# Hybrid layer kernel: V kept unsplit and split chunk by chunk, three ring slots for the remainders

## The chip, the cores and the metric

One core of a Trainium2 chip runs the whole layer in one launch. The metric is the device time of one execution in microseconds (us). The engines are named as in the profile: PE is the matrix engine (PEld its weight loads), DVE, ACT and POOL work on tiles, SP issues most of the DMAs. SBUF is the memory on the chip, PSUM the accumulators that PE writes, DRAM the memory outside.

## The reference, cut to what matters

A layer over 2048 rows of width 1024 in float32. `proj = x @ w_in` gives queries, keys, values and gates for four branches; stick-breaking attention is the first of them. For each head (4 heads of 128) and each block of 128 queries:

```
z      = q @ k^T * scale                       # 128 queries x keys up to the diagonal
log_1m = log_sigmoid(-z), 0 above the diagonal
w      = exp(log_sigmoid(z) + sum of log_1m over the later keys)
o      = w @ v
```

The kernel computes the same as products: the share of a key is sigmoid(z), the remainder is the running product of sigmoid(-z) over the later keys, w is share times remainder. The other branches (pooling, a gated recurrence, cross attention to a memory), the gated sum of the branches, `merged @ w_out` and a layer norm are untouched by the change.

## The kernel before, in words

Float32 products are made of three faster ones: every operand is split into a high part (a rounding copy, by ACT) and a low part (operand minus high, by DVE or POOL), and PE adds high x high, high x low and low x high (`pass3`, lines 821 to 825).

The rows are worked on in two halves of 1024 columns (`half`). Projections are made two tiles at a time: a pair `g` (36 in each half) is 14 pieces `i` of six matmuls of 512 columns. Pairs 0 to 7 of a half give the heads' q, k, v and gate; the odd pair of a head gives v. Every engine's program is written out by hand, and every engine walks the same list of pieces in the same order; semaphores tie them together.

**V before.** In the odd pair of a head, at pieces 10 and 12, PE turns half of V (4 transposes of 128x128 into a PSUM bank, `turn`, line 890), ACT copies the high part out (`values_hi`, line 1277), DVE makes the low part (`turned`, line 1755). SP stores both parts in `pk_v` in DRAM (`keep_values`). A chunk of 512 keys comes back with both parts as 512 KB in one DMA into `VC` (`load_v`, line 518), after the values product of the chunk before it has read `VC`.

**The attention.** `attention(half, h)` walks steps `s`, 12 a head in half 0 and 28 in half 1. A step is one block of 128 queries against one chunk of 512 keys (fewer on the diagonal); four steps make a group that reads one chunk of keys and one of values. In iteration `s` PE does `scores(s)` (into one of two PSUM banks), some pieces of projections of the next pairs as filling, in iterations 4n+7 and 4n+8 the two products with values of group n, and last `turned(s - 3)`, the transposes of the weights. The others, by iteration:

- ACT: the high part of the turned weights of step s-4 (line 1380), `shares(s)` (`KEEP` line 1366, `SHARE` line 1371), filling.
- DVE: `remainder(s - 1)`, the scan that writes `REST` (line 1901), the mask on diagonals (1890), the low part of the turned weights of step s-4 (1914), in one iteration of each head the first output (`Y<-AO,Y`, line 1921; iteration 9 in half 0, 17 in half 1), filling (among it lines 1746, 1777, 1784).
- POOL: `weights(s - 1)`, REST times SHARE in place (line 2390), filling (lines 2333, 2341, 2320).

`scores(s + 2)` writes the bank that the scan of step s reads (its first column stands in as the unused second operand) and waits for it: `wait_if(pe, scan_done, gs - 1)`. `REST` has four slots, one for each query block of the group; the scan of a step starts from the last element of its own slot, written four steps earlier, and waits until PE has turned the step before it in the same slot: `wait_if(dve, wt_done, gs - BLOCKS + 1)`.

Of the kernel before, what the change touches and what calls it, by code (L numbers as in the profile page):

```python
# [11 lines left out]
P = 128  # L12
# [70 lines left out]
TURN, TAIL = 3, 5  # L83
# [29 lines left out]
def first_step(half, h):  # L113
    return half * HEADS * NS[0] + h * NS[half]

# [60 lines left out]
def build(nc, xt, xrow, memt, w8, w4, wgate, wpool, prm, cst, ln_g, ln_b, out):  # L176
    with ExitStack() as ctx:
# [24 lines left out]
        B = R + 48.03125  # L202
# [23 lines left out]
        REST = at("REST", R + 32, [BLOCKS, C + 2])  # L226
        WTH = at("WTH", R + 40.03125, [2, BLOCKS, HALF], F32R)
        KC = [at(f"KC{i}", R + 48.03125 + 4 * i, [2, C], F32R) for i in range(2)]
        KEEP = at("KEEP", R + 56.03125, [2, C + 2])
        WTL = at("WTL", R + 60.0625, [2, BLOCKS, HALF], F32R)  # L230
        VC = at("VC", R + 68.0625, [BLOCKS, 2, P], F32R)
# [20 lines left out]
        LR_ = [at(f"LR{i}", R + k, [T]) for i, k in enumerate((28, 8, 52.0625))]  # L252
# [3 lines left out]
        LG = [at(f"LG{i}", R + 52.0625 + 4 * i, [T]) for i in range(2)]  # L256
        LA, LT = at("LA", R + 60.0625, [T]), at("LT", R + 64.0625, [T])
# [38 lines left out]
        pk_v = nc.dram_tensor("pk_v", (HEADS, P, SEQ // P, 2, P), F32).ap()  # L296
# [33 lines left out]
        v_kept = [sem("v_hi_kept"), sem("v_lo_kept")]  # L330
# [3 lines left out]
        v_tr, v_hi, v_blk = sem("v_tr"), sem("v_hi"), sem("v_blk")  # L334
# [122 lines left out]
        def _(sp):  # L457
# [35 lines left out]
            def keep_values(g):  # L493
                half, h = g // PAIRS, g % PAIRS // 2
                hh = half * HEADS + h
                for part, of in ((1, places(half, STL)[1]), (0, places(half, STL)[2])):
                    sp.wait_ge(v_blk, 2 * hh + 2)
                    sp.dma_start(pk_v[h, :, half * TB:(half + 1) * TB, part, :],
                                 of[:].bitcast(F32).rearrange("p (b m) -> p b m", m=P)).then_inc(v_kept[part], 16)
# [9 lines left out]
            def load_v(half, h, i):  # L509

                n, k = first_group(half, h) + i, STEPS[half][BLOCKS * i][1]
                if i == 0:
                    for kept in v_kept:
                        sp.wait_ge(kept, 16 * (half * HEADS + h + 1))
                    if h == 0:
                        wait_if(sp, o_out[1], 16 * 3 * half)
# [24 lines left out]
            def attention(half, h):  # L541
# [3 lines left out]
                for s in range(ns + TAIL + 1):  # L545
# [11 lines left out]
                    elif BLOCKS < s <= ns and s % BLOCKS == 0:  # L557
                        load_v(half, h, s // BLOCKS - 1)
# [260 lines left out]
        def _(pe):  # L819
# [16 lines left out]
            def piece(g, i, ks=(0, 1)):  # L836
# [9 lines left out]
                elif i == 0:  # L846
                    pe.wait_ge(a_lo, g + 1)
                    wait_if(pe, ad_done, 4 * (g - 1) + 2)
                    if 2 <= l <= 2 * HEADS and l % 2 == 0:
                        pe.wait_ge(v_blk, 2 * (half * HEADS + l // 2))  # L850
# [27 lines left out]
                if l < 2 * HEADS and l % 2 and i in (10, 12):  # L878
                    turn(g, 0 if i == 10 else 1)

            def turn(g, part):

                hh = g // PAIRS * HEADS + g % PAIRS // 2
                v, c = places(g // PAIRS, ST)[2], J[(g + 1) % 2]
                if part:
                    pe.wait_ge(v_blk, 2 * hh + 1)
                else:
                    pe.wait_ge(ad_done, 4 * g + 2)
                for j in range(4):
                    mm = nc.tensor.transpose(c[:, j * P:(j + 1) * P], v[:, (4 * part + j) * P:(4 * part + j + 1) * P],  # L890
                                             IDENT[:])
                mm.then_inc(v_tr, 1)
# [47 lines left out]
            def turned(half, h, s):  # L940
# [5 lines left out]
                n = C - a  # L946
                for b in range(n // P):
                    w = REST[:, j, n - P * (b + 1):n - P * b]
# [3 lines left out]
            def values(half, h, i):  # L952
# [6 lines left out]
                pe.wait_ge(v_in, 16 * (n + 1))  # L959
# [182 lines left out]
        def _(act):  # L1142
# [32 lines left out]
            def room(g, p):  # L1175
# [3 lines left out]
                if kind == "head":  # L1179
# [3 lines left out]
                    if i % 2 == 0 and p:  # L1183
                        wait_if(act, v_kept[1], 16 * hh)
# [4 lines left out]
                    elif i % 2:  # L1189
                        wait_if(act, v_kept[0], 16 * hh)  # L1190
                elif kind == "merge" and i >= 2:
                    gates_read(half, n, 2 * i + p - 4)
                elif kind == "merge" and n == 0:
                    if i == 0:
# [3 lines left out]
                        elif half or not p:  # L1198
                            act.wait_ge(k_kept, 32 * HEADS * (half + 1))
                            act.wait_ge(v_kept[1], 16 * HEADS * (half + 1))  # L1200
                        else:
                            act.wait_ge(v_kept[0], 16 * HEADS * (half + 1))
                    elif p:
                        act.wait_ge(w_done, S_END[half])
                    elif half:
                        act.wait_ge(v_kept[0], 16 * HEADS * (half + 1))
# [38 lines left out]
            def piece(g, i):  # L1245
# [24 lines left out]
                if g % PAIRS < 2 * HEADS and g % 2 and i in (10, 12):  # L1270
                    values_hi(g, 0 if i == 10 else 1)

            def values_hi(g, part):

                hh = g // PAIRS * HEADS + g % PAIRS // 2
                act.wait_ge(v_tr, 2 * hh + part + 1)
                nc.scalar.copy(places(g // PAIRS, STL)[2][:, part * C:(part + 1) * C], J[(g + 1) % 2][:]).then_inc(v_hi, 1)
# [121 lines left out]
            def attention(half, h):  # L1399
# [8 lines left out]
                for s in range(ns + TAIL + 1):  # L1408
                    if 0 <= s - TURN - 1 < ns:
                        turned_hi(half, h, s - TURN - 1)  # L1410
# [1146 lines left out]
```

## Time and profile before

| | us |
|---|---|
| median of 3 runs | 2293.88 (2293.3 to 2294.76) |
| the profiled execution | 2293.96 |
| its span in the trace | 2292.2 |
| PE busy | 2279.5 (99%) |
| DVE busy | 1444.4 (63%) |
| POOL busy | 1224.3 (53%) |
| ACT busy | 1060.2 (46%) |
| DMA moved | 297.84 MB, mean 130 GB/s |

The profiled execution has 1.8 us around its span and stands 0.1 us above the median. PE shows busy almost throughout, but its records overlap (matmuls are pipelined), so its pace is read from the starts of successive matmuls. Time of another engine counts only where PE waits for it. The attention takes the span from 79 to 285 us in half 0 and from 1144 to 1473 us in half 1.

### The profile page before, as it was taken

To read this page: it belongs to the slowest core of one execution; us is meant where nothing else is said; L and a number is where in the kernel's file an instruction comes from. 1 tells how busy PE (TensorE), PEld (TensorE's weight loads), DVE (VectorE), ACT (ScalarE), POOL (GpSimd) and SP (SyncE) were. 2 spreads that over 40 slices of the span, in tenths; PEclk is the share of its full clock that TensorE was granted. 3 is DMA by queue.
4 is the path that set the end of the run, shared out by engine and by line. 5 is a ranking of instruction groups with operands and counts; after the bars stand their busy time and mean duration, and the time that the engine had idled before them with its cause. 6 is when DMAs were issued, how large, how long until landed. Compare 5 with 4: busy or idle time off the path is not lost.

```text
span 2292.2 us, 29991 instructions
## 1 busy us (share of the span) xinstructions
PE 2279.5 (99%) x10824; PEld 1886.8 (82%) x10824; DVE 1444.4 (63%) x1658; ACT 1060.2 (46%) x1627; POOL 1224.3 (53%) x847
## 2 busy tenths in 40 slices
PE   9999999999999999999999999999999999999998
PEld 6888888888878888888888888888888778888887
DVE  7565542764496478568877777733854585486476
ACT  5555542343385255332576676632342583355220
POOL 1666643865456355435476566644863556456341
PEclk9999999999999999999999999999999999999999
DMA  6544422123334345373344543322133334354442
GB/s 234 187 159 158 139 83 97 55 83 129 113 104 133 134 124 148 105 284 138 108 159 139 165 156 124 125 92 78 56 120 124 92 103 134 130 156 132 152 161 83
DMA packets 114419, 297.84 MB, mean 130 GB/s; under 512 B 11232, under 2 KB 41056, under 8 KB 113248
## 3 DMA queue, kind: packets, MB, share of 16 engines
q1 hardware_dynamic: 112544, 290.68, 38.6%
q10 hardware_dynamic: 1728, 5.24, 0.7%
q8 instruction: 87, 1.43, 0.3%
q14 instruction: 60, 0.49, 0.1%
HBM read 216.19 MB, written 71.30 MB: 125 GB/s over the span
## 4 chain that ended last, share of the span: by engine, by line
PE 97%; DVE 1%; DMA 1%; issue 0%; DVEq 0%
PE J L823 21%; PE J L825 21%; PE J L824 21%; PE ZZ L995 8%; PE AO L995 8%; PE ZZ L825 2%; PE ZZ L824 2%; PE ZZ L823 2%; PE AO L825 2%; PE AO L824 2%; PE AO L823 2%; PE AO L949 1%; PE JX L949 1%; PE ZZ L1030 1%; PE JX L825 1%; PE JX L823 1%
## 5 line engine op out<-in xcount | busy, mean ns | idle before, releaser
L2341 POOL TENSOR_TENSOR WLS<-SR,WHS 128x512 fp32r<-128x512 f32 x264 | 414.3, 1588 | 110.1 <-ACT WHS L1161 102.5
L823 PE MATMUL J<-XBH,WHS 128*128 128x512 f32 x1152 | 452.3, 393 | 0.0
L825 PE MATMUL J<-XBH,WLS 128*128 128x512 f32 x1152 | 449.1, 390 | 0.0
L824 PE MATMUL J<-XBL,WHS 128*128 128x512 f32 x1152 | 448.9, 390 | 0.0
L823 PE MATMUL J<-XBH,WH 128*128 128x512 f32 x864 | 340.3, 394 | 0.4 <-DVE WL L1764 0.2
L825 PE MATMUL J<-XBH,WL 128*128 128x512 f32 x864 | 337.0, 390 | 0.0
L824 PE MATMUL J<-XBL,WH 128*128 128x512 f32 x864 | 336.8, 390 | 0.0
L825 PEld LDWEIGHTS J<-XBH,WLS 128*128 128x128 f32 x1152 | 216.2, 188 | 46.0
L824 PEld LDWEIGHTS J<-XBL,WHS 128*128 128x128 f32 x1152 | 216.4, 188 | 43.6 <-issue 0.2
L823 PEld LDWEIGHTS J<-XBH,WHS 128*128 128x128 f32 x1152 | 216.4, 188 | 43.5 <-issue 0.2
L2333 POOL TENSOR_TENSOR SR<-RAW 128x512 f32<-128x512 f32 x71 | 100.6, 1417 | 269.8 <-DMA RAW<-w 230.8
L1746 DVE TENSOR_TENSOR ST<-J,ST 128x512 f32<-128x512 f32 x160 | 109.5, 685 | 209.1 <-PE J L825 162.2
L2390 POOL TENSOR_TENSOR REST<-REST,SHARE 128x512 f32<-128x512 f32 (+3 forms) x160 | 165.6, 1037 | 119.7 <-DVE REST L1901 116.1
L2407 POOL TENSOR_TENSOR BL<-BRAW,BH 128x512 fp32r<-128x512 f32 x64 | 89.3, 1401 | 220.2 <-ACT BH L1429 220.0
L823 PEld LDWEIGHTS J<-XBH,WH 128*128 128x128 f32 x864 | 162.3, 188 | 40.1 <-issue 7.3
L1161 ACT CAST WHS<-SR 128x1024 fp32r<-128x1024 f32 x144 | 151.3, 1051 | 93.5 <-POOL SR L2333 92.4
L825 PEld LDWEIGHTS J<-XBH,WL 128*128 128x128 f32 x864 | 162.2, 188 | 34.8
L824 PEld LDWEIGHTS J<-XBL,WH 128*128 128x128 f32 x864 | 162.3, 188 | 31.8 <-issue 0.2
L2333 POOL TENSOR_TENSOR SR<-SR,RAW 128x512 f32<-128x512 f32 x71 | 105.6, 1488 | 120.4 <-PE J L825 118.4
L1243 ACT COPY ST<-J 128x512 f32<-128x512 f32 x160 | 93.8, 590 | 125.1 <-PE J L825 122.4
L1901 DVE TENSOR_TENSOR_SCAN REST<-KEEP,REST,ZZ 128x513 f32<-128x513 f32 x96 | 122.8, 1279 | 25.5 <-ACT SHARE L1371 24.6
L2333 POOL TENSOR_TENSOR SR<-RAW,SR 128x512 f32<-128x512 f32 x71 | 102.3, 1441 | 51.3 <-PE J L825 50.3
(305 smaller groups left out, 4753.3 us busy)
## 6 DMA issues: line engine op xcount, KB each, us to landing
RAW<-w SPq DMA_DIRECT2D x144, 512.0 KB, 3.7
pk_m<-MB SPq DMA_DIRECT2D x56, 512.0 KB, 5.0
MB<-pk_m SPq DMA_DIRECT2D x48, 512.0 KB, 3.9
KC<-pk_k SPq DMA_DIRECT2D x40, 512.0 KB, 5.4
VC<-pk_v SPq DMA_DIRECT2D x40, 512.0 KB, 4.4
BRAW<-w SPq DMA_DIRECT2D x64, 256.0 KB, 5.0
XRAW<-xt SPq DMA_DIRECT2D x8, 1024.0 KB, 12.6
pk_v<-STL SPq DMA_DIRECT2D x16, 512.0 KB, 5.0
```

The source lines that it names most:

```text
L823: nc.tensor.matmul(to, wh, xh, start=first, stop=True, skip_group_check=True)
L824: nc.tensor.matmul(to, wh, xl, start=False, stop=True, skip_group_check=True)
L825: return nc.tensor.matmul(to, wl, xh, start=False, stop=True, skip_group_check=True)
L995: mm = nc.tensor.matmul(BR[p][c][:], w[p][:, k, :], y[k][:, c * C:(c + 1) * C], start=(k == 0 and m == 0), stop=(k == KB - 1 and m == 2))
L1161: nc.scalar.copy(WHS[:, k, :], SR[:, k, :]).then_inc(w_hi, 1)
L1243: nc.scalar.copy(dest(g)[p][:, c * C:(c + 1) * C], J[(g + bank) % 2][:]).then_inc(cp_done, 1)
L1746: V_.tensor_tensor(d, bank[:], d, ALU.add).then_inc(ad_done, 1)
L1901: V_.tensor_tensor_scan(REST[:, j, 0:n + 1], KEEP[:, gs % 2, 0:n + 1], ZB[gs % 2][:, 0:1].broadcast_to([P, n + 1]), 1.0 if diag else REST[ ...
L2333: G_.tensor_tensor(SR[:, 4 * j:4 * j + 4], a, b, op).then_inc(s_raw, 1)
L2341: low = G_.tensor_tensor(WLS[:, k, :], SR[:, k, :], WHS[:, k, :].bitcast(F32), ALU.subtract)
L2390: G_.tensor_tensor(w, w, SHARE[gs % 2][:, 0:n], ALU.mult).then_inc(w_done, 1)
L2407: G_.tensor_tensor(BL[f % 2][:], BRAW[f % 2][:], BH[f % 2][:].bitcast(F32), ALU.subtract).then_inc(b_lo, 1)
```

## The change

V is turned by DVE in blocks of 32x32 (`turn_values`, both halves of V at piece 10) from SBUF to SBUF, and stored unsplit in one DMA. The rest of the turn is done by the DMAs that bring a chunk back: four of 64 KB, in runs of 128 floats, into the new tile `VRAW` (2 KB a partition). ACT and DVE then split the chunk into `VC` in iteration 4n+5 of the attention: `values_hi` behind `shares` on ACT, `values_lo` behind `turned_lo` on DVE, both reading `VRAW` in runs of 32. `TURN` stays 3 and the split of the turned weights stays at s-4, now named `SPLIT`. Room for `VRAW` comes from `REST`, which has three slots in place of four; a step's slot is shifted by one element every three steps, so that the last element of four steps earlier, from which the scan starts, survives. The transposes, ACT copies and DVE subtractions of V on the odd pairs, and PE's waits for them, are gone. Some tiles move by up to 0.0625 KB.

```diff
+SLOTS, SHIFTS = 3, 5
+def rest_place(half, s):
+    c, k, j, a, diag, end = STEPS[half][s]
+    return SHIFTS - (s - (ENDS[half][c - 1] + 1 if c else 0)) // SLOTS + a
-        REST = at("REST", R + 32, [BLOCKS, C + 2])
+        REST = at("REST", R + 32, [SLOTS, SHIFTS + C + 1])
+        VRAW = at("VRAW", R + 38.09375, [C])
+        def chunk_moved():
+            return VRAW[:].rearrange("p (i b r) -> p b i r", i=GROUPS, b=BLOCKS)
+        def chunk_part(part):
+            return VC[:, :, part, :].rearrange("p b (i r) -> p b i r", i=GROUPS)
 SP, keep_values
-                for part, of in ((1, places(half, STL)[1]), (0, places(half, STL)[2])):
-                    sp.wait_ge(v_blk, 2 * hh + 2)
-                    sp.dma_start(pk_v[h, :, half * TB:(half + 1) * TB, part, :], ...
+                sp.wait_ge(v_tr, NC * (hh + 1))
+                sp.dma_start(pk_v[h, :, half * TB:(half + 1) * TB, :], ...
 SP, load_v
-                wait_if(sp, pv_done, 2 * n)
-                sp.dma_start(VC[:].bitcast(F32), pk_v[h, :, BLOCKS * (k ^ 1):BLOCKS * (k ^ 1) + BLOCKS]).then_inc(v_in, 16)
+                wait_if(sp, vc_lo, n)
+                for q in range(GROUPS):
+                    rows = pk_v[h, :, GROUPS * (k ^ 1) + q].rearrange("(i x) m -> x i m", i=GROUPS)
+                    to = VRAW[SQUARE * q:SQUARE * (q + 1)].rearrange("x (i m) -> x i m", i=GROUPS)
+                    sp.dma_start(to, rows).then_inc(v_in, 16)
 SP, attention
-                    elif BLOCKS < s <= ns and s % BLOCKS == 0:
-                        load_v(half, h, s // BLOCKS - 1)
+                    elif BLOCKS < s < ns and s % BLOCKS == BLOCKS - 1:
+                        load_v(half, h, s // BLOCKS)
 PE: turn() and its calls at pieces 10 and 12 gone; turned() reads REST[:, gs % SLOTS, ...]
 PE, values
-                pe.wait_ge(v_in, 16 * (n + 1))
+                pe.wait_ge(vc_lo, n + 1)
 ACT
+            def values_hi(half, h, i):
+                n = first_group(half, h) + i
+                act.wait_ge(v_in, 16 * GROUPS * (n + 1))
+                wait_if(act, pv_done, 2 * n)
+                ...
+                nc.scalar.copy(chunk_part(0), chunk_moved()).then_inc(vc_hi, 1)
 ACT, attention, behind shares(half, h, s)
+                    if TAIL <= s < ns + BLOCKS and s % BLOCKS == 1:
+                        values_hi(half, h, s // BLOCKS - 1)
 DVE
+            def turn_values(g):
+                hh = g // PAIRS * HEADS + g % PAIRS // 2
+                dve.wait_ge(ad_done, 4 * g + 2)
+                dve.wait_ge(k_kept, 32 * (hh + 1))
+                _, to, v = places(g // PAIRS, ST)
+                for c in range(NC):
+                    t = slice(c * C, (c + 1) * C)
+                    V_.transpose(to[:, t].rearrange("p (q b x) -> p b q x", q=GROUPS, b=BLOCKS),
+                                 v[:, t].rearrange("p (b n) -> p b n", b=BLOCKS)).then_inc(v_tr, 1)
+            def values_lo(half, h, i):
+                n = first_group(half, h) + i
+                dve.wait_ge(vc_hi, n + 1)
+                V_.tensor_tensor(chunk_part(1), chunk_moved(), chunk_part(0).bitcast(F32), ALU.subtract).then_inc(vc_lo, 1)
 DVE, remainder
-                wait_if(dve, wt_done, gs - BLOCKS + 1)
-                V_.tensor_tensor_scan(REST[:, j, 0:n + 1], ...
-                                      1.0 if diag else REST[:, j, before:before + 1], ...
+                wait_if(dve, wt_done, gs - SLOTS + 1)
+                V_.tensor_tensor_scan(REST[:, gs % SLOTS, first:first + n + 1], ...
+                                      1.0 if diag else REST[:, (gs - BLOCKS) % SLOTS, before:before + 1], ...
 DVE, attention, behind turned_lo(half, h, s - SPLIT), ahead of output() and of the filling
+                    if TAIL <= s < ns + BLOCKS and s % BLOCKS == 1:
+                        values_lo(half, h, s // BLOCKS - 1)
```

The waits that ACT's filling had on the two stored parts of V (`room`) now name the one store or the turn.

## Rows read from the trace of the kernel before

**Rows 1.** The page, part 1: busy us, share of span, instructions

```profile
PE 2279.5 (99%) x10824; PEld 1886.8 (82%) x10824; DVE 1444.4 (63%) x1658; ACT 1060.2 (46%) x1627; POOL 1224.3 (53%) x847
```

**Rows 2.** The page, part 4: chain that ended last, by engine

```profile
PE 97%; DVE 1%; DMA 1%; issue 0%; DVEq 0%
```

**Rows 3.** Timeline, PE, V's first turn: start, us, engine, line, operation, tiles

```profile
68.00 0.39 PE L824 MATMUL J<-XBL,WHS 128*128 128x512 f32 x1
68.23 0.40 PE L825 MATMUL J<-XBH,WLS 128*128 128x512 f32 x1
68.47 0.60 PE L890 MATMUL J<-IDENT,ST 128*128 128x128 f32 x4
68.82 0.48 PE L823 MATMUL J<-XBH,WHS 128*128 128x512 f32 x1
69.14 0.39 PE L824 MATMUL J<-XBL,WHS 128*128 128x512 f32 x1
```

**Rows 4.** Groups by line and shape: xcount | busy us, mean ns | idle before

```profile
L890 PE MATMUL J<-IDENT,ST 128*128 128x128 f32 x64 | 9.8, 275 | 0.0
L1277 ACT CAST STL<-J 128x512 fp32r<-128x512 f32 x16 | 9.5, 593 | 8.9 <-PE J L890 8.9
L1755 DVE TENSOR_TENSOR STL<-J,STL 128x512 fp32r<-128x512 f32 x16 | 11.0, 685 | 4.3 <-ACT STL L1277 4.2
L1166 ACT CAST WH<-RAW 128x512 fp32r<-128x512 f32 x72 | 44.3, 616 | 35.2 <-PE J L825 35.2
L2125 DVE STREAM_TRANSPOSE PB<-PR 128x1024 f32<-128x1024 f32 x12 | 14.9, 1246 | 0.4
```

**Rows 5.** Waits of PE: who waited for what, us, times, longest

```profile
PE AO L823 <- DMA VC<-pk_v: 0.8, 3, 0.3
```

**Rows 6.** Timeline, half 1, head 3, step 17

```profile
1441.38 0.59 ACT L1371 ACTIVATE SHARE<-ZZ 128x512 f32<-128x512 f32 x1
1441.41 0.68 DVE L1921 TENSOR_TENSOR Y<-AO,Y 128x512 f32<-128x512 f32 x1
1442.01 1.28 DVE L1901 TENSOR_TENSOR_SCAN REST<-KEEP,REST,ZZ 128x513 f32<-128x513 f32 x1
1443.46 0.48 PE L823 MATMUL ZZ<-KC,QH 128*128 128x512 f32 x1
1444.62 0.36 PE L823 MATMUL AO<-WTH,VC 128*128 128x256 f32 x1 [0.21 <-DMA VC<-pk_v]
```

**Rows 7.** Timeline, half 1, head 1, steps 17 and 18

```profile
1271.64 0.59 ACT L1371 ACTIVATE SHARE<-ZZ 128x512 f32<-128x512 f32 x1
1272.27 1.28 DVE L1901 TENSOR_TENSOR_SCAN REST<-KEEP,REST,ZZ 128x513 f32<-128x513 f32 x1 [0.28 <-ACT SHARE L1371]
1273.70 1.09 POOL L2390 TENSOR_TENSOR REST<-REST,SHARE 128x512 f32<-128x512 f32 x1 [1.72 <-DVE REST L1901]
1273.92 1.42 DVE L1777 TENSOR_TENSOR WL<-RAW,WH 128x512 fp32r<-128x512 f32 x1
1275.11 0.48 PE L823 MATMUL ZZ<-KC,QH 128*128 128x512 f32 x1
1275.26 1.27 DVE L1901 TENSOR_TENSOR_SCAN REST<-KEEP,REST,ZZ 128x513 f32<-128x513 f32 x1
1276.91 0.48 PE L823 MATMUL ZZ<-KC,QH 128*128 128x512 f32 x1
```

**Rows 8.** The instructions of line 1777: ns min, median, max

```profile
L1777 DVE TENSOR_TENSOR WL<-RAW,WH x71: 676/1221/1815, 25.9 to 2159.5; 128x512 fp32r<-128x512 f32 x71
```

**Rows 9.** Busy time of each engine, half 1, head 3

```profile
1403.00:1473.00 70.00, 69.39 (x425) 60.16 (x424) 53.41 (x71) 47.70 (x94) 44.30 (x40) 1.00 0.38 123
```

**Rows 10.** DMA issues: KB each, median us from issue to landing

```profile
VC<-pk_v SPq DMA_DIRECT2D x40, 512.0 KB, 4.4
PR<-pk_t SPq DMA_DIRECT2D x64, 128.0 KB, 3.4
```

**Rows 11.** Waits of SP: who waited for what, us, times, longest

```profile
SPq L518 <- PE AO L825: 232.8, 32, 13.0
```

More of the change, by code:

```diff
@@ L251, in build @@
         LI_ = [at(f"LI{i}", R + k, [T]) for i, k in enumerate((0, 4, 44.03125))]
[L252 removed]
+        LR_ = [at(f"LR{i}", R + k, [T]) for i, k in enumerate((28, 8, 52.125))]
         LI, LR = [LI_[i] for i in (0, 1, 0, 2)], [LR_[i] for i in (0, 1, 0, 2)]
@@ L255, in build @@
         LU_ = [at(f"LU{i}", R + k, [4 + T]) for i, k in enumerate((48.03125, 40))]
-        LG = [at(f"LG{i}", R + 52.0625 + 4 * i, [T]) for i in range(2)]
-        LA, LT = at("LA", R + 60.0625, [T]), at("LT", R + 64.0625, [T])
+        LG = [at(f"LG{i}", R + 52.125 + 4 * i, [T]) for i in range(2)]
+        LA, LT = at("LA", R + 60.125, [T]), at("LT", R + 64.125, [T])
         WGR = at("WGR", R + 68.25, [P])
@@ L495, in keep_values @@
                 hh = half * HEADS + h
-                for part, of in ((1, places(half, STL)[1]), (0, places(half, STL)[2])):
-                    sp.wait_ge(v_blk, 2 * hh + 2)
-                    sp.dma_start(pk_v[h, :, half * TB:(half + 1) * TB, part, :],
-                                 of[:].bitcast(F32).rearrange("p (b m) -> p b m", m=P)).then_inc(v_kept[part], 16)
+                sp.wait_ge(v_tr, NC * (hh + 1))
+                sp.dma_start(pk_v[h, :, half * TB:(half + 1) * TB, :],
+                             places(half, ST)[1][:].rearrange("p (b m) -> p b m", m=P)).then_inc(v_kept, 16)
             def load_k(half, h, i):
@@ L877, in piece @@
                     mm.then_inc(pr_done, 1)
[L878 to L892, printed above, removed]
             def pair(g, inside={}, first=0):
@@ L945, in turned @@
                 wait_if(pe, wt_lo, gs - 1)
-                n = C - a
+                n, first = C - a, rest_place(half, s)
                 for b in range(n // P):
-                    w = REST[:, j, n - P * (b + 1):n - P * b]
+                    w = REST[:, gs % SLOTS, first + n - P * (b + 1):first + n - P * b]
                     mm = nc.tensor.transpose(TB_[gs % 2][:, b * P:(b + 1) * P], w, IDENT[:])
@@ L1205, in room @@
                     elif half:
-                        act.wait_ge(v_kept[0], 16 * HEADS * (half + 1))
+                        act.wait_ge(v_tr, NC * HEADS * (half + 1))
                     else:
@@ L1269, in piece @@
                     shared(g, 1, 0, 0, 6)
[L1270 to L1277, printed above, removed]
+            def values_hi(half, h, i):
+                n = first_group(half, h) + i
+                act.wait_ge(v_in, 16 * GROUPS * (n + 1))
+                wait_if(act, pv_done, 2 * n)
+                if h == 0 and i == 0:
+                    wait_if(act, o_out[1], 16 * 3 * half)
+                nc.scalar.copy(chunk_part(0), chunk_moved()).then_inc(vc_hi, 1)
             def split_keys(g):
@@ L1800, in piece @@
                     rest_of_sums(g + 1, False)
-                if l < 2 * HEADS and l % 2 and i in (10, 12):
-                    turned(g, 0 if i == 10 else 1)
+                if l < 2 * HEADS and l % 2 and i == 10:
+                    turn_values(g)
             def pair(g, after={}, first=0):
@@ L1945, in attention @@
                         piece(*pieces.pop(0))
-                    if 0 <= s - TURN - 1 < ns:
-                        turned_lo(half, h, s - TURN - 1)
+                    if 0 <= s - SPLIT < ns:
+                        turned_lo(half, h, s - SPLIT)
+                    if TAIL <= s < ns + BLOCKS and s % BLOCKS == 1:
+                        values_lo(half, h, s // BLOCKS - 1)
                     if s == ENDS[half][0] + TAIL + 1:
@@ L2388, in weights @@
                 pool.wait_ge(scan_done, gs + 1)
-                w = REST[:, j, 0:n]
+                first = rest_place(half, s)
+                w = REST[:, gs % SLOTS, first:first + n]
                 G_.tensor_tensor(w, w, SHARE[gs % 2][:, 0:n], ALU.mult).then_inc(w_done, 1)
```

53 lines of the change are left out of this document (22 added, 31 removed).

## The prediction

> **What bounds the kernel now.** I read the page first: PE is busy 99% of the span [rows 1] and the chain that ended last runs on PE for 97% of it [rows 2]. So PE's program, in its order, sets the time: a matmul taken out of it shortens the kernel by its own pace, and work on another engine counts only where PE then waits. Second, PE's waits: of those that the change touches there is one group, 3 waits of 0.8 us in all for the chunk of values [rows 5]. Third, the timeline of the attention, for the question on which the answer hangs: how early is DVE's scan of a step done before `scores` two steps later wants its bank? I call that the margin. In half 1, head 1, step 17 the scan starts at 1272.27, takes 1.28 and `scores(19)` starts at 1275.11: margin 1.56 [rows 7]. In head 3, step 17: 1443.46 - (1442.01 + 1.28) = 0.17 [rows 6]. Head 3 of half 1 is the tight place, since it has less filling; DVE is busy there 53.4 of 70 us [rows 9].
>
> **The change, part by part.**
>
> *PE's turns of V go.* 64 transposes in 16 groups of 4 [rows 4]. Their price is not 4 x 275 ns, since matmuls overlap. Successive 512-column matmuls start 0.23 apart (68.00 to 68.23). From 68.23 to the second matmul behind the transposes, 69.14, are 0.91 where two paces would be 0.46: 0.45 for a group [rows 3]. That holds for 13 groups; 3 stand directly before transposes of weights and read 0.32 in the same way. Gain: 13 x 0.45 + 3 x 0.32 = 6.8 us.
>
> *The chunk's late arrival goes.* The load waited for the values product of the chunk before it and was needed three iterations later. By the recorded waits that is 0.8 us [rows 5]; by PE's starts, which show more (1444.62 comes 0.38 later than the pace allows, the others 0.45 and 0.48), 1.3. I take 1.3, because starts are what PE loses; both ends are small. The new load is released once the chunk before it is split (iteration 4n+1) and needed in 4n+5, four iterations or some 9 us on. Landing takes 4.4 for 512 KB in one DMA and 3.4 for the nearest thing to the new form, DMAs of 128 KB on 32 partitions [rows 10]; with four issues I put it at 3.4 to 7, inside the 9. SP isn't late: at the old place it stood waiting for PE 232.8 us over 32 chunks, 7 us each [rows 11], and the new place is one iteration earlier in its order, ahead of the loads of keys and weights. Cost 0.
>
> *DVE turns V.* 16 transposes of 128x512, at half of 1.246 us each, for 16 subtractions at 0.685 and 16 ACT copies at 0.593 [rows 4]: no more than before, at places where only the store waits. 0.
>
> *Three slots.* The scan of step s now waits for `turned(s - 3)`, the last thing in PE's iteration s, where before that of s-4 had long run. Comparing both in the 160 steps, 98 scans would start later, by up to 3.2 us (the largest in half 0, with margins above 4). After subtracting that, every margin stays above zero (smallest 0.05, untouched by it), as PE has a whole iteration between `turned(s - 3)` and `scores(s + 2)`. Alone: 0 to 2 us; I take 0 alone, and let it stand in the delays below, which mostly exceed it.
>
> *The split of a chunk, in front of a scan.* This is the cost. In iteration 4n+5 ACT does `shares(s)`, then the copy. DVE in the same iteration comes to `values_lo` behind `turned_lo`, and waits there for the copy; queued behind it are the output, the filling and `remainder(s)`, the scan of that very step, on which POOL's weights and `scores(s + 2)` wait. Before, the scan followed `SHARE` at once (1272.23 to 1272.27 [rows 7]). Now come in between the ACT copy, 0.62 (the mean of line 1166 [rows 4]), two hand-overs of 0.03 and DVE's subtraction d. In the iteration of the output (0.68, [rows 6]) that no longer fits in DVE's idle time before the share is ready and is added, and so is filling that stood ready.
>
> For d: the old subtraction read PSUM and took 0.685 throughout [rows 4]. The new one reads two tiles of SBUF, like line 1777, which took 0.68 to 1.82, median 1.22 [rows 8]. Which of them is told by POOL: line 1777 started at 1273.92 under POOL's instruction of 1273.70 to 1274.79, and took 1.42, which is 0.87 left of POOL's and 0.55 [rows 7]. So d = 0.68 with POOL idle, else 0.55 plus the rest of POOL's instruction, up to 1.8. POOL is idle at the place in question in 20 of the 32 cases, because it is waiting for that scan.
>
> The Trainium skill, "SBUF — State Buffer", section "Who interferes with whom", says that a DVE instruction with two SBUF inputs contends with a GpSimd instruction that reads SBUF, and that the loser blocks for the whole instruction. Line 1777 under POOL agrees [rows 7]. A flat 0.68, as the replaced subtraction has, would make the sum below 5.7 us less.
>
> Loss in a step = 0.68 (copy and hand-overs) + d + what is pushed behind it - margin, where positive, read for all 32 steps 4n+5 as in the two worked here. Half 1, head 3, step 17: 1441.97 + 0.68 + 0.68 + 0.68 + 1.28 = 1445.3 against 1443.46: 1.8 [rows 6]. Head 1, step 17: 1272.23 + 0.68 + 0.68 + 0.68 + 1.28 = 1275.55 against 1275.11: 0.4 [rows 7]. The rest, same reading:
> - half 0: step 9 of heads 0 to 2: 0.3 each; head 3, steps 5 and 9: 0.4 and 1.1. Sum 2.4.
> - half 1, head 0: steps 5, 9, 21 (POOL busy, d = 1.8): 0.8 each; step 17: 1.1. Sum 3.5.
> - half 1, heads 1 and 2: step 5 (POOL busy) 0.8, step 17 0.4, step 21 (key subtraction of 1.8 behind it) 0.7. Sum 4.0 for both.
> - half 1, head 3: steps 5, 9, 17, 21, 25: 1.4, 1.4, 1.8, 0.4, 2.7. Sum 7.7.
> Together 17.6; the steps left out have margin enough.
>
> Then the step after. In head 1 the scan of step 17 ends 2.0 late; the low part (0.53) and line 1777 follow, and the scan of step 18, at 1275.26 before with its `scores(20)` at 1276.91 and a margin of 0.38, comes to 1278.1 to 1278.7. PE is itself 0.45 later, so it waits 0.7 to 1.3 more [rows 7]. I take 1.0 for each of heads 1 and 2; elsewhere the margin behind is about as large as the one before. Loss 17.6 + 2.0 = 19.6.
>
> *Sum*, on the profiled execution: 2293.96 - 6.8 - 1.3 + 19.6 = 2305.5 (that execution is 0.1 above the median, which I let go).
>
> **The rivals.**
>
> *A. Faster: the split hides.* If ACT and DVE reach the split before the share of that step matters, so that the scan isn't held (DVE idle before many scans speaks for room; the written order speaks against, as the copy stands behind `shares(s)` and the scan behind the subtraction), only the gains and at most the ring's 2 us are left: 2293.96 - 8.1 + 0 to 2 = 2285.9 to 2287.9. It decides where copy, subtraction and output together stay under the margin.
>
> *B. A draw.* The delays are there but small: d = 0.68 throughout and no step after: 17.6 - 5.7 = 11.9 of loss, and if the turns give back another 0.5 of waits around them, 2297.3; with half of the losses caught by slack that I don't see, 2291.3. Around 2294. POOL's idleness in 20 of 32 cases speaks for part of it, head 3's margins of 0.05 to 0.2 against.
>
> *C. DVE becomes the bound.* 28 steps in head 3 of half 1: 53.4 of 70 us busy [rows 9], plus seven splits at up to 1.8 makes 66. Then delays don't drain in four steps, and d = 1.8 in the 20 idle cases too adds 1.1 each, 22, less some 7 of margin left in the roomy ones: 19.6 + 15 = 34.6 of loss, 2320.5. Against: the rows on POOL.
>
> *D. The chunk lands late.* If four DMAs of 512-byte runs took over 9 us, ACT would stand in `values_hi` with the turned weights queued behind: 1 us a chunk is 32 us, 2325 or more. Landing times speak against [rows 10].
>
> The Trainium skill, "DMA: Bandwidth & Descriptors", section "Specifications", gives 512 B as the least transfer for line rate, so by it D does not happen; no row before has this form.
>
> **How the numbers follow.** The forecast 0.63, A 0.12, B 0.15, C 0.07, D 0.03. The forecast's own range is 2299 to 2314. With most of B and some of C: 2291 to 2316. A measurement of this kernel tells 0.2%, 4.6 us, from no change: 2289.3 to 2298.5. Faster 0.12 (A), the same 0.15 (B), slower 0.73.
>
> **What would show it.** In the changed kernel's trace: no line for V's transposes on PE. New waits of PE at `scores` (ZZ<-KC) for DVE's scan, once per chunk, longest in half 1, head 3 (about 8 of the 20 us), hardly any in heads 0 to 2 of half 0. DVE's low part of VC idle before it for ACT's copy, 0.68 or 1.2 to 1.8 long by POOL. No wait of PE for `VC`, none of ACT for VRAW worth naming. The span between 285 and 1144 as long as before. Wrong if PE's waits for the scan stay under 5 us in sum, or if they stand at steps other than 4n+5 (then it is the ring), or if ACT waits for VRAW.

## The result: 20.9 us slower, 9.4 more than forecast

| | before | after |
|---|---|---|
| median (4 runs each) | 2294.08 (2293.3 to 2294.76) | 2315.14 (2314.91 to 2317.65) |
| profiled execution | 2293.96 | 2314.91 |
| its span | 2292.2 | 2313.1 |

The ratio is 1.0094, 95% interval 1.0077 to 1.0112. Forecast was 2305.5, with an own range of 2299 to 2314 and, with most of B and some of C, 2291 to 2316. The sign held and the wide range did, by 0.9 us; the own range was missed by 1.1. Of the medians the difference is 21.1, of the spans 20.9; the balance below is made for the spans.

**How it is split.** Every matmul of after has its partner before (the transposes of V left out). I take for each the start after minus the start before. Where this difference rises, PE lost time there; where it falls, PE gained. Summed by what the matmul at the rise belongs to:

| place | forecast | measured |
|---|---|---|
| around the transposes of V that are gone | -6.8 | -7.0 |
| products with values | -1.3 | -1.0 |
| `scores`, all | +19.6 | +19.7 |
| ends of heads 0, 1, 2 of half 0 | 0 | +7.2 |
| all else (before 60 us +0.6, after 1495 us +1.7, between -0.2) | 0 | +2.1 |
| sum | 11.5 | 20.9 (its terms, rounded, give 21.0) |

**The profile after.** The page, part 1, answers to [rows 1]: 64 fewer instructions on PE, 40 more on DVE, and DVE 22.4 us busier.

```profile
PE 2281.2 (99%) x10760; PEld 1884.5 (81%) x10760; DVE 1466.8 (63%) x1698; ACT 1069.4 (46%) x1651; POOL 1240.6 (54%) x847
```

PE still shows 99%, while it lost 27 us at two kinds of places (19.7 and 7.2): the busy share does not tell a loss of 1%. The list of the chain by engine [rows 2] names only 37% of the span after, so I don't read it.

The waits of after (engine, line, tile, what it waited for: us in all, times, longest) answer to [rows 5]:

```profile
PE ZZ L839 <- DVE REST L1911: 13.7, 14, 2.6
PE J L839 <- ACT ST L1242: 5.4, 3, 2.5
PE AO L839 <- DVE PTL L2153: 0.6, 1, 0.6
ACT VC L1277 <- DMA VRAW<-pk_v: 12.4, 5, 3.9
DVE VC L1765 <- ACT VC L1277: 29.2, 35, 3.9
DVE REST L1911 <- ACT SHARE L1371: 31.2, 38, 2.3
```

The first line is the forecast one: `scores` waits for the scan. The starts show 19.7 where the list has 13.7: a matmul's start can slip with no listed wait before it. The second and the fourth line were not forecast: PE waits for a copy out of PSUM by ACT, three times, and ACT had waited for the chunk. The fourth is one of the signs that the prediction named for itself being wrong ("or if ACT waits for VRAW").

Groups by line and shape, after (xcount | busy us, mean ns | idle before), answer to [rows 4]:

```profile
L1765 DVE TENSOR_TENSOR VC<-VRAW,VC 128x512 fp32r<-128x512 f32 x40 | 39.0, 976 | 29.3 <-ACT VC L1277 29.2
L1277 ACT CAST VC<-VRAW 128x512 fp32r<-128x512 f32 x40 | 24.8, 621 | 12.4 <-DMA VRAW<-pk_v 12.4
L1758 DVE STREAM_TRANSPOSE ST<-ST 128x512 f32<-128x512 f32 x16 | 10.4, 685 | 0.0
```

The new transposes cost what the subtractions cost that they replace, mean 685 both. The chunk's subtraction in single values (ns min/median/max), which answers to [rows 8]:

```profile
L1765 DVE TENSOR_TENSOR VC<-VRAW,VC x40: 681/1006/1829, 93.4 to 1489.3; 128x512 fp32r<-128x512 f32 x40
```

**The forecast kind of loss**, half 1, head 3, step 25, in the timeline (start, us, engine, line, operation, tiles, in brackets the idle time before it):

```profile
1477.55 0.59 ACT L1371 ACTIVATE SHARE<-ZZ 128x512 f32<-128x512 f32 x1
1478.03 0.62 ACT L1277 CAST VC<-VRAW 128x512 fp32r<-128x512 f32 x1
1478.68 1.02 DVE L1765 TENSOR_TENSOR VC<-VRAW,VC 128x512 fp32r<-128x512 f32 x1 [0.39 <-ACT VC L1277]
1479.10 1.73 POOL L2354 TENSOR_TENSOR WLS<-SR,WHS 128x512 fp32r<-128x512 f32 x1
1479.62 1.75 DVE L1786 TENSOR_TENSOR WL<-RAW,WH 128x512 fp32r<-128x512 f32 x1
1481.30 1.27 DVE L1911 TENSOR_TENSOR_SCAN REST<-KEEP,REST,ZZ 128x513 f32<-128x513 f32 x1
1482.62 0.50 PE L839 MATMUL ZZ<-KC,QH 128*128 128x512 f32 x1 [2.65 <-DVE REST L1911]
```

Share and copy are done at 1478.65; the chunk's subtraction and a weight's subtraction (1.02 and 1.75, mostly beside POOL) stand before the scan; `scores` follows the scan's end, 1482.57, by 0.05. The rise here is 2.8, forecast 2.7. (The same `scores` loses 1.11 with the three slots alone, see e1_ring: the two causes overlap here, and this row doesn't part them.)

**The kind that was not forecast**, end of head 2 of half 0:

```profile
228.05 2.15 DVE L1793 TENSOR_TENSOR STL<-ST,KHT 128x1024 fp32r<-128x1024 f32 x1
230.23 0.38 SPq L507 DMA_DIRECT2D pk_k<-KHT  x1
230.65 1.44 SPq L507 DMA_DIRECT2D pk_k<-STL  x1
232.13 2.85 SPq L534 DMA_DIRECT2D VRAW<-pk_v  x4
...
239.26 0.62 ACT L1277 CAST VC<-VRAW 128x512 fp32r<-128x512 f32 x1 [3.94 <-DMA VRAW<-pk_v]
239.79 0.58 ACT L1242 COPY ST<-J 128x512 f32<-128x512 f32 x1
240.42 0.50 PE L839 MATMUL J<-XBH,WHS 128*128 128x512 f32 x1 [2.51 <-ACT ST L1242]
```

SP's order puts the two stores of the next head's keys ahead of the load of the last chunk. They wait for DVE's low part of the keys (done 230.20), and take 0.38 and 1.44 to issue; the four loads take another 2.85. The chunk lands at 239.2, 9 us after the keys were ready to store. ACT stands 3.94 in `values_hi`, with the copy that empties a PSUM bank queued behind it, and PE stands behind that copy. The same happens at 122.7 and 181.0; the three rises are 1.77, 1.63 and 2.75, 6.15 together. The rest of the 7.2 comes right after the third.

Two more chunks were late. At 290.96 ACT stood 1.19 with no loss of PE. In step 21 of head 3, half 1, it stood 1.48; the load had been issued at 1462.10, directly behind one of weights (1461.70):

```profile
1467.65 0.62 ACT L1277 CAST VC<-VRAW 128x512 fp32r<-128x512 f32 x1 [1.48 <-DMA VRAW<-pk_v]
1468.31 0.69 DVE L1765 TENSOR_TENSOR VC<-VRAW,VC 128x512 fp32r<-128x512 f32 x1 [1.99 <-ACT VC L1277]
1470.25 0.49 PE L839 MATMUL ZZ<-KC,QH 128*128 128x512 f32 x1 [1.53 <-DVE REST L1911]
```

This loss, 1.78, stands in the row `scores` of the balance.

The windows of after behind the longest stall (us from, to, length, PE, PEld, DVE, ACT, POOL busy, granted clock, DMA share, GB/s):

```profile
240.40:242.00 1.60, 1.58 (x6) 1.21 (x7) 1.41 (x3) 1.40 (x2) 0.12 (x1) 0.92 0.84 302
242.00:245.00 3.00, 3.00 (x15) 2.96 (x14) 1.25 (x3) 0.59 (x1) 2.38 (x2) 0.50 0.27 111
245.00:248.00 3.00, 3.00 (x16) 2.53 (x15) 1.04 (x3) 1.08 (x2) 0.98 (x1) 0.97 0.00 0
```

After this stall (2.75 by the starts, 2.51 as a listed wait) the granted clock was 0.50, that is 1.2 of 2.4 GHz, for some 3 us.

### The profile page after: what moved, and what is told of

Read it like the earlier page. It is cut to its first block and busy times, and to the rows that moved or that the text cites. A ratio compares the mean times of both kernels' runs of the same rounds, so it can differ in the third digit from the quotient of the medians.

```text
span 2313.1 us, 30069 instructions
## 1 busy us (share of the span) xinstructions
PE 2281.2 (99%) x10760; PEld 1884.5 (81%) x10760; DVE 1466.8 (63%) x1698; ACT 1069.4 (46%) x1651; POOL 1240.6 (54%) x847
## 3 DMA queue, kind: packets, MB, share of 16 engines
q8 instruction: 87, 1.43, 0.3%
## 5 line engine op out<-in xcount | busy, mean ns | idle before, releaser
L2346 POOL TENSOR_TENSOR SR<-RAW 128x512 f32<-128x512 f32 x71 | 107.2, 1510 | 272.0 <-DMA RAW<-w 233.1
L2404 POOL TENSOR_TENSOR REST<-REST,SHARE 128x512 f32<-128x512 f32 (+3 forms) x160 | 171.2, 1071 | 139.4 <-DVE REST L1911 131.7
L2346 POOL TENSOR_TENSOR SR<-SR,RAW 128x512 f32<-128x512 f32 x71 | 104.5, 1471 | 119.1 <-PE J L841 116.5
```

The source lines that it names most:

```text
L2346: G_.tensor_tensor(SR[:, 4 * j:4 * j + 4], a, b, op).then_inc(s_raw, 1)
L2404: G_.tensor_tensor(w, w, SHARE[gs % 2][:, 0:n], ALU.mult).then_inc(w_done, 1)
```

## The experiments

All times are medians. The kernel before ran beside each: 2293.94, 2294.10 and 2294.01 in the three batches (13, 14 and 21 runs), so that kernels of different batches can be compared to some 0.2 us. "Scores" is read from the one profiled execution of each kernel: the time from the start before to the start of `scores`, less that matmul's usual pace, summed where it is over 0.13. By this count the changed kernel has 17.3 and the kernel before 0. "Head ends" is the loss at the pieces of projections, of which the kernel before has 4.3 and the changed one 9.3.

| kernel | median (lowest to highest) | ratio to before, 95% | scores | head ends |
|---|---|---|---|---|
| e1_ring | 2296.81 (2296.14 to 2297.66) | 1.0012 (1.0002 to 1.0021) | 2.5 | 3.9 |
| e2_double | 2346.02 (2345.49 to 2352.45) | 1.0232 (1.0217 to 1.0248) | 45.1 | 12.5 |
| e3_next | 2318.62 (2317.49 to 2319.48) | 1.0106 (1.0091 to 1.0121) | 6.3 | 8.3 |
| e4_early | 2306.31 (2304.6 to 2307.03) | 1.0051 (1.0034 to 1.0068) | 15.7 | 3.9 |
| e5_pool | 2294.42 (2293.34 to 2295.46) | 1.0 (0.9991 to 1.001) | 5.9 | 3.5 |
| e6_first | 2313.73 (2311.35 to 2315.15) | 1.0085 (1.007 to 1.01) | 16.4 | 8.2 |
| e7_first_early | 2303.01 (2302.33 to 2304.17) | 1.004 (1.0025 to 1.0055) | 14.1 | 3.3 |
| e8_store | 2303.14 (2300.96 to 2303.71) | 1.0038 (1.0024 to 1.0053) | 12.8 | 3.3 |
| e9_pool_first | 2292.4 (2290.88 to 2293.36) | 0.9991 (0.9982 to 1.0) | 4.2 | 3.3 |
| e10_psum_work | 2295.92 (2294.2 to 2296.55) | 1.0008 (0.9999 to 1.0017) | 7.1 | 3.3 |

**e1_ring: the kernel before with three slots, nothing else.**

```diff
-                wait_if(dve, wt_done, gs - BLOCKS + 1)
+                wait_if(dve, wt_done, gs - SLOTS + 1)
```

> The kernel before with nothing changed but REST: three slots with shifted places, the scan waiting for the turn three steps back. Theory (the split in front of the scan and the late chunk are the price): margins absorb the later scans, 0 to 2 us more than before, 2294 to 2296, PE's waits for the scan under 2 us in sum. Rival (the ring is the price): the waits of PE at scores stay as in the changed kernel, 17 us, 2308 or more.

2.9 us slower (2296.81 - 2293.94), and PE waits where it never had:

```profile
PE ZZ L831 <- DVE REST L1910: 1.8, 4, 0.9
```

So the ring costs some 3 us alone, above the bound of 0 to 2 in the forecast (and of 2294 to 2296 here). Its losses stand at four `scores` of half 1: step 20 of heads 1 and 2 (0.55, 0.36), steps 10 and 27 of head 3 (0.45, 1.11). Before the last one, the scan of step 24 waits for PE's turn of the weights, where before it waited 0.29 for `SHARE`; behind it line 1785 finds more of POOL's instruction still to run and takes 1.48 where it had taken 0.99, and the scan of step 25 comes 1.1 later in PE's program than before:

```profile
1460.77 1.28 DVE L1910 TENSOR_TENSOR_SCAN REST<-KEEP,REST,ZZ 128x513 f32<-128x513 f32 x1 [1.38 <-PE AO L957]
1462.55 1.48 DVE L1785 TENSOR_TENSOR WL<-RAW,WH 128x512 fp32r<-128x512 f32 x1
1465.28 0.51 PE L831 MATMUL ZZ<-KC,QH 128*128 128x512 f32 x1 [0.95 <-DVE REST L1910]
```

**e2_double: the changed kernel with DVE's subtraction of the chunk done twice.**

```diff
-                V_.tensor_tensor(chunk_part(1), chunk_moved(), ...).then_inc(vc_lo, 1)
+                for made in (vc_mid, vc_lo):
+                    V_.tensor_tensor(chunk_part(1), chunk_moved(), ...).then_inc(made, 1)
+                    if made is vc_mid:
+                        dve.wait_ge(vc_mid, n + 1)
```

> The changed kernel with DVE's subtraction of the chunk (values_lo) made twice, one after the other. Theory: it stands in front of the scan, so that each step 4n+5 pays 0.75 us less what margin it has left: over the 32 steps some 15 us, with the steps after them 15 to 19: 2330 to 2334. Rival (ring or late chunk decide, DVE has room for it): under 2319.

30.9 slower than the changed kernel; 15 to 19 were expected, so the direction held and the size did not. (Its profiled span, 2350.7, lies some 6 us above what its median suggests, with a granted clock of 0.993 where the other three runs had 0.996 and 0.997; what is read from its trace is that much too long in all.) 80 subtractions take 79.6 us, so 40.6 us of DVE work were added and 30.9, three quarters, came out as time:

```profile
PE ZZ L839 <- DVE REST L1914: 39.5, 30, 3.2
```

Work in front of the scan has a price, and the second portion costs more than the first: in the trace 28 of the added us are at `scores`, where the first had cost 17.3. That the margins are then used up is the reading that fits; no run varies a margin.

**e3_next: DVE's subtraction one iteration later.**

```diff
-                    if TAIL <= s < ns + BLOCKS and s % BLOCKS == 1:
+                    if TAIL <= s < ns + BLOCKS and s % BLOCKS == 2:
                         values_lo(half, h, s // BLOCKS - 1)
```

> The changed kernel with DVE's subtraction one iteration later (4n+6, behind turned_lo, so behind the scan of step 4n+5 and in front of that of 4n+6); all else the same. Theory: the scan of 4n+5 is no longer held by ACT's copy, PE's losses at scores fall from 17 to some 3 us: 2299 to 2304. Rival (DVE has too much work in all, wherever it stands): 2311 or more.

A miss. `scores` lose only 6.3, but the low part is now late for the products with values:

```profile
PE AO L839 <- DVE VC L1765: 10.1, 20, 1.1
PE ZZ L839 <- DVE REST L1911: 5.2, 4, 1.5
```

The starts of the values products lose 15.9 where the changed kernel has 0.8. Of the two places tried on DVE neither is free: ahead of one scan it delays `scores`, one iteration on it delays the values.

**e4_early: the load one iteration earlier in SP's order, ahead of the key stores.**

```diff
-                    elif BLOCKS < s < ns and s % BLOCKS == BLOCKS - 1:
+                    elif BLOCKS < s < ns and s % BLOCKS == BLOCKS - 2:
                         load_v(half, h, s // BLOCKS)
```

> The changed kernel with the load of a chunk one iteration earlier in SP's order (4n+2 in place of 4n+3). In half 0 the last chunk of a head is then issued ahead of the stores of the next head's keys, behind which it stands now. Theory: the PE stalls of 1.8, 1.6 and 2.7 us at the ends of heads 0 to 2 of half 0, and the slow stretch at half clock behind the longest, go: 7 us less, 2308. Rival (ACT is late there by its own work, not by the chunk): 2314 to 2316.

8.8 faster than the changed kernel (2315.14 - 2306.31). No wait of ACT for VRAW is left, nor of PE for ACT; pieces lose 3.9 and `scores` 15.7 (17.3 before). The 1.6 less at `scores` are nearly all step 21 of head 3, where the chunk is in time now: 0.29 lost for 1.78. Start by start the two profiled executions differ by 8.2: 7.8 between 60 and 250 us, 1.5 at step 21 and 0.8 at 2113.6 are gained; 0.5 are lost before 60 us and 1.5 behind the stall at 1473.8, where the granted clock now falls (0.50 from 1476 to 1478) and in the changed kernel did not.

**e5_pool: e4_early, and the chunk's low part made by POOL, in iteration 4n+5 behind `weights(s - 1)`.** The edit in part; the call moves from DVE's loop to POOL's.

```diff
+            def values_lo(half, h, i):               # POOL's program, DVE's is gone
+                n = first_group(half, h) + i
+                pool.wait_ge(vc_hi, n + 1)
+                G_.tensor_tensor(chunk_part(1), chunk_moved(), ...).then_inc(vc_lo, 1)
```

> The changed kernel with the earlier load and with the subtraction on POOL, in iteration 4n+5 behind weights(4n+4), and none on DVE. Theory: the scan of 4n+5 is free, POOL is late with the weights of that step by about 1 us, which has 1.7 us or more of room before PE turns them; filling on POOL and DVE instructions with two SBUF inputs are held a little: 2292 to 2298. Rival (POOL's wait for ACT's copy holds the weights and by them SHARE two steps on): 2303 or more.

11.9 faster than e4_early, level with the kernel before. Some 1.5 of it is the fall of the clock in e4_early's trace, which doesn't occur here. POOL takes longer for the same subtraction, and PE's waits for the scan come to 4.9 (12.1 in e4_early):

```profile
L2392 POOL TENSOR_TENSOR VC<-VRAW,VC x40: 1276/1292/2277, 93.5 to 1468.1; 128x512 fp32r<-128x512 f32 x40
PE ZZ L839 <- DVE REST L1905: 4.9, 6, 1.4
```

**e6_first and e7_first_early: ACT's copy of the chunk ahead of `shares`;** e6 on the changed kernel, e7 on e4_early.

```diff
+                    if TAIL <= s < ns + BLOCKS and s % BLOCKS == 1:
+                        values_hi(half, h, s // BLOCKS - 1)
                     if s < ns:
                         shares(half, h, s)
-                    if TAIL <= s < ns + BLOCKS and s % BLOCKS == 1:
-                        values_hi(half, h, s // BLOCKS - 1)
```

> The changed kernel with ACT's copy of the chunk (values_hi) in front of shares(s) in iteration 4n+5 in place of behind it; DVE's subtraction and the load stay where they are. Theory: the copy then runs while PE makes the scores, the subtraction is done before the share is, and the scan of 4n+5 follows SHARE again: PE's losses at scores fall from 17 to the ring's 2.5 and some 2 for a share that comes 0.25 us later: 2301 to 2304. Rival (what holds the scans is DVE's amount of work): 2311 or more.

> The last one and the earlier load of the chunk (4n+2) together. Theory: the two losses are separate and add up, the load gave 8.8: 2293 to 2296. Rival (they share a cause): 2299 or more.

Both miss: 1.4 under the changed kernel and 3.3 under e4_early, where 11 to 14 and 10 to 13 were expected. The reason is in the subtraction's line, first e4_early, then e7_first_early:

```profile
L1765 DVE TENSOR_TENSOR VC<-VRAW,VC 128x512 fp32r<-128x512 f32 x40 | 38.3, 958 | 17.1 <-ACT VC L1277 17.0
```

```profile
L1765 DVE TENSOR_TENSOR VC<-VRAW,VC 128x512 fp32r<-128x512 f32 x40 | 51.8, 1296 | 0.4
```

The wait for the copy went, 17.1 to 0.4, and the subtraction grew from 38.3 to 51.8: DVE is held 55.4 before and 52.2 after. Ahead of the share, DVE meets POOL at `weights`. The timeline of e7 at the same step 25 of head 3:

```profile
1466.44 1.28 POOL L2404 TENSOR_TENSOR REST<-REST,SHARE 128x512 f32<-128x512 f32 x1 [2.16 <-DVE REST L1911]
1466.80 1.48 DVE L1765 TENSOR_TENSOR VC<-VRAW,VC 128x512 fp32r<-128x512 f32 x1
1467.69 1.71 POOL L2354 TENSOR_TENSOR WLS<-SR,WHS 128x512 fp32r<-128x512 f32 x1
1468.19 1.75 DVE L1786 TENSOR_TENSOR WL<-RAW,WH 128x512 fp32r<-128x512 f32 x1
1469.87 1.27 DVE L1911 TENSOR_TENSOR_SCAN REST<-KEEP,REST,ZZ 128x513 f32<-128x513 f32 x1
1471.19 0.50 PE L839 MATMUL ZZ<-KC,QH 128*128 128x512 f32 x1 [2.63 <-DVE REST L1911]
```

The copy is early and yet PE waits as long as in the changed kernel, 2.63 against 2.65. In e6_first the chunks are late as well, ACT waits 14.9 for them in 8 places.

**e8_store: e7, and V's store ahead of the load of weights at piece 12.** The edit in part; the old call at piece 13 goes.

```diff
                 elif i == 12 and l + 2 < PAIRS:
+                    if head and l % 2:
+                        keep_values(g)
                     load_w(g + 2, 0)
```

> The last one, and V's store issued by SP ahead of the weight load of piece 12 in place of behind it. Theory: at the start of half 1 ACT waited for that store and PE with it 1.4 us (at the scores of step 2); this goes: 1.4 less than the last. Rival (ACT is late there for another reason): the same as the last.

The stall at the start of half 1 (1.42 at 1156.0 in the changed kernel, where ACT waited 1.49 for the store of V) is gone from the trace, `scores` lose 12.8 instead of 14.1, but the median is the same (2303.14 against 2303.01). The two traces, one of each kernel, show start by start where it went: 1.4 is gained at 1146, and 1.5 is lost between 1471 and 1474, behind the stall of step 25, where the granted clock falls in e8_store and stays full in e7. Windows behind that stall, first e7_first_early, then e8_store:

```profile
1471.10:1473.00 1.90, 1.81 (x12) 1.67 (x13) 1.90 (x4) 0.81 (x2) 1.10 (x1) 1.00 0.84 273
```

```profile
1470.10:1472.00 1.90, 1.84 (x6) 1.55 (x7) 1.90 (x4) 0.30 (x1) 1.09 (x1) 0.56 0.73 257
1472.00:1474.00 2.00, 2.00 (x12) 2.00 (x12) 0.45 (x1) 0.78 (x2) 1.70 (x2) 0.56 1.21 211
```

The other runs fit: four of e8's five have a mean clock of 0.998, where e7's have 0.999 and 1.0, and the fifth, with 0.999, took 2300.96.

**e9_pool_first: e5_pool with e6's and e8's edits**, POOL's subtraction as in e5.

> All of it together: three slots, early load, ACT's copy of the chunk ahead of the shares, the subtraction on GpSimd (one per chunk, behind the weights of the chunk's step, none on VectorE), and the store of ST ahead of the head's RAW load. Theory (only what stands in front of VectorE's scan costs; GpSimd has room): the subtraction begins earlier on GpSimd, so the losses at 1161.5 and 1421.1 (0.58 and 1.45) mostly go and the store takes off some 1.5 at 1144: 2294.4 - 1.5 - 1.5 = 2291.4, 2.7 under the kernel before. Rival (the shares, now a copy later, wait longer for ScalarE, and the weights of the next step are pushed back by GpSimd's 1.28): 2294 to 2298, no gain over the kernel before. Decided by 2293.

2292.4, 1.6 below the kernel before and 22.7 below the changed one. It lies between theory and rival, nearer the theory. Only the stall for the store went; of the two losses that the earlier copy was to remove, 0.58 is 0.54 now and 1.45 is 1.45, so the copy's place had no part in them (the second stands at one of e1's four steps). The stall for the store is e8's edit. The interval touches 1.0: a gain over the kernel before is likely and small.

**e10_psum_work: e5_pool, and `turned_lo` done twice on DVE in iteration 4n+5, work that reads PSUM.** The edit in part.

```diff
                     if 0 <= s - SPLIT < ns:
+                        if s % BLOCKS == 1 and TAIL <= s:
+                            turned_lo(half, h, s - SPLIT, wt_mid)
                         turned_lo(half, h, s - SPLIT)
```

> The kernel with the subtraction on GpSimd and the early load, plus, in each step in which VectorE had subtracted the chunk in the changed kernel, one more copy of the same size of work on VectorE that reads PSUM (a turned_lo done twice, 0.69 alone), with no wait for ScalarE. It repeats work and changes no value. Theory A (VectorE's time in front of the scan costs, whatever kind): 0.7 to 0.9 in front of the scan where the subtraction with two SBUF operands had 1.29 (the median with the copy first), so about 4 to 6 of the 8.6 between that kernel (2303.0) and this one's base (2294.4) come back: 2298.5 to 2300.5. Theory B (only the stretching against GpSimd's weights costs, VectorE's own 0.69 fits in the slack): 2294.5 to 2296.5. Theory C (any further instruction there costs as much as the subtraction did): 2302 or more.

1.5 slower than e5_pool: inside theory B's 2294.5 to 2296.5. The added 40 are 24 of 512 columns and 16 of 256, and take 23.3 us (59.9 - 43.4 and 13.3 - 6.5). Rows of e10:

```profile
L1920 DVE TENSOR_TENSOR WTL<-AO,WTH 128x512 fp32r<-128x512 f32 x88 | 59.9, 680 | 16.9 <-ACT WTH L1380 16.1
L1920 DVE TENSOR_TENSOR WTL<-AO,WTH 128x256 fp32r<-128x256 f32 x32 | 13.3, 415 | 2.1 <-ACT WTH L1380 1.4
```

Their mean of 680 is that of e5 (678), and none of line 1920 took over 694 ns, whatever POOL did meanwhile.

**The experiments side by side.** Held time of DVE is the subtraction's busy time and its wait for the copy; the kernels without late chunks first:

| | e5_pool | e10 | e7 | e4 | changed | e2 |
|---|---|---|---|---|---|---|
| DVE held, us | 0 | 23.3 | 52.2 | 55.4 | 68.3 | 112.3 |
| lost at scores, us | 5.9 | 7.1 | 14.1 | 15.7 | 17.3 | 45.1 |

The time held in front of the scan orders all six. The first 23 us cost 1.2, the next 30 cost 7 to 9, 13 more up to the changed kernel 1.6, and the last 44 cost 28 (in the execution that is 6 us too long). In the last two columns part of the held time lies at the head ends, where PE waits for something else, and all but e10 and e5_pool contain the split on DVE, so that this is one series and no law. Whether the kind of work matters by itself is not shown: e10's pieces are 0.68 or 0.42 long, the stretched subtractions 1.3 in the mean, and no run had PSUM work of that length.

## Why the forecast was right in sign and 9.4 short

**Turns of V, -6.8:** measured -7.0. **Late values, -1.3:** -1.0. Both right. **DVE turns V, 0:** a transpose took 685 ns, not the 623 that half of 1.246 us gives, which cost nothing; but "at places where only the store waits" failed once. At the start of half 1 ACT waits 1.49 for V's store, where it had waited 0.89 before, and PE loses 1.42; e8 takes that away.

**The split in front of the scan, +19.6:** measured +19.7. Step by step it agrees less well, and that the sums agree is luck. Of the 19.7, 1.4 is the store of V and 1.5 the late chunk at step 21 of head 3, neither of them the split, and at four `scores` the ring's 2.5 overlap with it; the split as priced gave 16.8 or less:

| | forecast | measured |
|---|---|---|
| half 0, heads 0, 1, 2 | 0.3 each | 0.29, 0.30, 0.28 |
| half 0, head 3 | 1.5 | 2.27 |
| half 1, head 0 | 3.5 | 3.20, of it 1.5 at step 2 |
| half 1, heads 1, 2, the step after included | 3.0 each | 2.16 each |
| half 1, head 3 | 7.7 | 9.03 |

Within head 1 the step after the one with the output lost 1.43 (forecast 1.0), the step itself 0.53 (0.4) and steps 5 and 21 nothing (0.8 and 0.7). In head 3 steps 5, 9, 17, 21 and 25 lost 1.12, 1.13, 1.58, 1.78 and 2.82 (1.4, 1.4, 1.8, 0.4, 2.7). (The parts forecast for heads 1 and 2, 0.8, 0.4 and 0.7, add to 1.9 and not to 2.0 each: the prediction's 17.6 should be 17.4.) The steps named are most of those that lose; the 1.78 of step 21 is the late chunk, and without it, in e4_early, the step lost 0.29. For d the formula was right and the reading of POOL was not: I had POOL idle in 20 of the 32 steps (d = 0.68) and d = 1.8 in the other 12. Measured, 6 of the 32 took under 0.72, one over 1.6, and most about 1.0, as the subtraction starts under the end of a POOL instruction. The two errors partly cancel: mean 0.95, where the forecast had 1.10. The 1.5 at step 2 of head 0 is V's store, issued at 1148.70.

That d is 0.55 plus the rest of POOL's instruction held: in e7 it began 0.92 before POOL's end, 1467.72, and took 1.48. All 40 subtractions of the changed kernel follow the rule within 0.08, under 0.72 where POOL was idle at their start; the two longest, 1.83 and 1.82 at 180.46 and 268.05, began together with an instruction of POOL of 1.28 and 1.29. The Trainium skill, "SBUF — State Buffer", section "Who interferes with whom", says that a DVE instruction with two SBUF inputs contends with a GpSimd instruction that reads SBUF, and that one with at most one SBUF input, outside the modes that use two ports, does not. The traces agree with both: line 1765 took 0.68 to 1.83 us by the rest of POOL's instruction, line 1920 in e10, with one input in PSUM, at most 694 ns.

**The ring, 0 (0 to 2):** e1 shows 2.9 alone. The step taken, that every margin stays above zero since PE has an iteration between `turned(s - 3)` and `scores(s + 2)`, failed at four steps. In the changed kernel it has no sum of its own: part of what I booked as the step after (1.43 in head 1) stands where e1 alone lost 0.55, and the 2.82 of step 25 in head 3 where e1 alone lost 1.11. In e5_pool, without the split on DVE, the same four `scores` lose 0.64, 0.44, 1.45 and 1.14; in e9_pool_first they are, with one of 0.54, all that is left.

**The load's new place, 0:** this step failed, at the sentence "SP isn't late: ... the new place is one iteration earlier in its order, ahead of the loads of keys and weights". It looked at SP's waits in general [rows 11] and at loads, not at what SP is asked to issue between the two places at the end of a head: the key stores, which wait for DVE. And it counted nothing for issuing four DMAs. The issues in single values (ns min/median/max) in after:

```profile
L534 SPq DMA_DIRECT2D VRAW<-pk_v x160: 302/432/2456, 80.1 to 1483.3; - x160
```

and their size and landing, which answers to [rows 10]:

```profile
VRAW<-pk_v SPq DMA_DIRECT2D x160, 64.0 KB, 3.5
```

A landing of 3.5 is inside the 3.4 to 7 assumed; SP's order made five of the 40 chunks late, three of them behind the key stores. Rival D had the mechanism (ACT stands in `values_hi` with other copies behind it), but at every chunk and for another cause. The step is worth 7.2 in the balance, 1.5 more inside `scores`, and 8.8 by e4's median; the missing 9.4 are these 7.2 and the 2.1 of "all else".

**The rivals.** A (hidden) fell with 17.3 at `scores`, and B (a draw) with it: it asked for d = 0.68 throughout and no step after, and got a median of 1.01 and 1.43 and 1.25 at the steps after. C asked for d = 1.8 in idle cases too and 2320.5; the median of 1.01 speaks against it, though 2315.1 lies nearer to its number than to the forecast. So the wide range held by what it had kept for B and C, and the time came near its upper end by neither.

**What stays open.** The 1.7 us lost after 1495 us lie in work that the change does not touch; 0.8 stands at one matmul (2113.6) behind DVE's line 2153, the rest is spread. The 0.8 is not the change of addresses alone: e2, e3, e4, e7 and e8 have the same addresses, and their traces have no wait of PE for line 2153. What brings it on is open. A store of V ahead of the weights' load without the early copy was not tried, nor a ring of four slots with the new split, for which there is no room.

## What to carry to other kernels

Price added work on a side engine by the time that it holds the engine in front of what the critical engine waits for, and compare it with the margin of each step: the first 23 us on DVE cost 1.2 here, the last 44 some 28. Moving an instruction that waits to an earlier place doesn't help if there it runs beside another engine's instruction and is stretched by it; giving the same work to the engine with slack on that chain did (11.9 us). And when a load moves, read the issuing queue between its old and its new place instruction by instruction: stores with waits of their own stood there, and the late chunks cost 8.8. When an edit removes a stall in the trace and the time stays, look at the granted clock behind the other stalls before calling the edit useless.

## What the runs showed of the hardware

- One of the four 64 KB loads occupied SP 0.43 us in the median and up to 2.46, against 0.32 and 0.37 for the load of 512 KB in the kernel before. After a store of 512 KB (1.44 to issue) the four took 2.85.
- After a stall of 2.75 us (by the starts) at 240.4 the granted clock went to 0.50 and cost about 1 us more. Not each stall brings that: after 2.82 at 1482.6 the clock stayed 1.00, and after 1.77 and 1.63 at 122.7 and 181.0 too. The same stall of step 25, 2.8 long in each kernel, was followed by a fall in e4_early (0.50) and e8_store (0.56), at 1.5 us each, and by none in the changed kernel and e7_first_early.
- The same subtraction of 128x512 floats from two SBUF tiles took 0.68 to 1.83 us on DVE, by what was left of POOL's instruction when it began, and 1.28 to 2.28 on POOL.
